# HGRN2 heads with one burst of all eight levels, and other places for splits, rests and table loads

## The reference

```python
q, fz, i, g = jnp.split(h @ w_in, [HG_FDIM, 2 * HG_FDIM, 2 * HG_FDIM + D_MODEL], axis=-1)
f = lb + (1.0 - lb) * jax.nn.sigmoid(fz)
log_f = jnp.log(jnp.maximum(f, HG_F_MIN))
k = (1.0 - lb) * jax.nn.sigmoid(-fz)
q = jax.nn.silu(q.astype(f32))
# per head, 8 heads of 128, with a state S of 128 x 128
b = jnp.cumsum(gc, axis=2)
A = jnp.einsum('bhtk,bhtsk,bhsk->bhts', qc, jnp.exp(rel), kc)     # rel = b[t] - b[s], causal
o = einsum('bhtk,bhkv->bhtv', qc * jnp.exp(b), S) + einsum('bhts,bhsv->bhtv', A, vc)
S = jnp.exp(b_last)[..., None] * S + einsum('bhsk,bhsv->bhkv', kc * jnp.exp(b_last - b), vc)
return rms_norm(o * jax.nn.sigmoid(g), g_norm) @ w_out, S
```

## Time and profile before

| | |
|---|---|
| Time, median of 3 runs (lowest, highest) | 3158.94 us (3158.48, 3159.76) |
| The profiled execution: time, span | 3158.79 us, 3157.2 us |
| Busy: PE, DVE, ACT, POOL | 97%, 61%, 37%, 4% |
| Mean granted clock of TensorE | 0.990 |

### The profile page before, as it was taken

How to read it: one execution, slowest core, us unless ns; L and a number is a source line. 1 busy time by engine, 2 the same in 40 slices (tenths; PEclk the granted TensorE clock), 3 DMA queues, 4 the chain that set the end, 5 groups by cost and what they waited for, 6 DMA issues and landing times.

```text
span 3157.2 us, 76452 instructions
## 1 busy us (share of the span) xinstructions
PE 3052.8 (97%) x31972; PEld 2858.8 (91%) x31972; DVE 1917.8 (61%) x3409; ACT 1172.0 (37%) x1971; POOL 131.4 (4%) x247
## 2 busy tenths in 40 slices
PE   8999999999999999998999998999999999999998
PEld 7998999999888999998897777999999998899998
DVE  6777654456676554555547887654555777664454
ACT  4333322223555322224536665322223333422222
POOL 0000000001332000000000000000000000000000
PEclk9999999999999999999999999999999999999999
DMA  3222222223443222222120000222222222222222
GB/s 131 102 95 70 95 87 90 84 101 99 137 129 114 88 86 94 85 97 82 61 75 12 25 26 25 87 87 93 87 95 85 89 88 99 79 84 97 80 94 74
DMA packets 104596, 269.00 MB, mean 85 GB/s; under 512 B 12802, under 2 KB 45954, under 8 KB 104146
## 3 DMA queue, kind: packets, MB, share of 16 engines
q1 hardware_dynamic: 91346, 228.54, 21.8%
q0 software_dynamic: 13056, 37.64, 3.5%
HBM read 247.61 MB, written 18.52 MB: 84 GB/s over the span
## 4 chain that ended last, share of the span: by engine, by line
PE 86%; DVE 7%; ACT 3%; DVEq 2%; issue 1%; DMA 0%; ACTq 0%; SPq 0%
PE ps L671 24%; PE ps L680 14%; PE ps L682 9%; PE ps L683 9%; PE ps L684 9%; PE ps L681 7%; PE ps L1171 3%; PE ps L1149 2%; PE ps L764 1%; PE ps L1181 1%; PE ps L997 1%; PE ps L831 1%; PE ps L1269 1%; PE ps L858 0%; PE ps L768 0%
## 5 line engine op out<-in xcount | busy, mean ns | idle before, releaser
L671 PE MATMUL ps<-arena_r 128*128 128x272 f32 x6768 | 929.8, 295 | 42.3 <-DVE arena_r L2196 19.1
L671 PEld LDWEIGHTS ps<-arena_r 128*128 128x128 f32 x6768 | 875.9, 191 | 79.5 <-issue 52.0
L1597 ACT ACTIVATE arena_r<-ring 128x1024 fp32r<-128x1024 f32 (+1 forms) x240 | 275.1, 1146 | 835.0 <-PE ps L684 820.9
L680 PE MATMUL ps<-hb_r,arena_r 128*128 128x480 f32 x1408 | 537.3, 382 | 3.4 <-DVE arena_r L2228 3.0
L682 PE MATMUL ps<-hb_r,arena_r 128*128 128x304 f32 x1408 | 427.4, 304 | 0.0
L684 PE MATMUL ps<-hb_r,arena_r 128*128 128x304 f32 x1408 | 425.9, 302 | 0.0
L683 PE MATMUL ps<-hb_r,arena_r 128*128 128x304 f32 x1408 | 425.6, 302 | 0.0
L681 PE MATMUL ps<-hb_r,arena_r 128*128 128x240 f32 x1408 | 384.0, 273 | 0.0
L2228 DVE TENSOR_TENSOR arena_r<-ring,arena_r 128x1024 fp32r<-128x1024 f32 (+1 forms) x240 | 318.4, 1327 | 49.4 <-ACT arena_r L1597 49.4
L2262 DVE TENSOR_TENSOR arena<-ps,rstd 128x544 f32<-128x544 f32 x176 | 127.5, 724 | 333.8 <-PE ps L684 333.5
L682 PEld LDWEIGHTS ps<-hb_r,arena_r 128*128 128x128 f32 x1408 | 264.6, 188 | 42.1
(11 more groups left out here) (447 smaller groups left out, 4407.6 us busy)
## 6 DMA issues: line engine op xcount, KB each, us to landing
ring<-in_w_up SPq DMA_DIRECT2D x176, 512.0 KB, 3.4
ring<-in_w_mix SPq DMA_DIRECT2D x112, 512.0 KB, 3.5
ring<-in_w_down SPq DMA_DIRECT2D x64, 704.0 KB, 4.1
arena<-in_hg_s POOLq DMA_DIRECT2D x16, 512.0 KB, 3.7
out_hg_so<-arena POOLq DMA_DIRECT2D x16, 512.0 KB, 2.9
ring<-in_w_hgout SPq DMA_DIRECT2D x16, 512.0 KB, 3.5
arena<-in_cache_k SPq DMA_DIRECT2D x128, 64.0 KB, 1.9
arena<-in_cache_v POOLq DMA_DIRECT2D x128, 64.0 KB, 2.2
```

Source lines behind the costliest of these rows:

```text
L671: mm = pe.matmul(PS[:, 2 * a + hf, 0:HALF], part[:, ws], rhs[:, o:o + HALF], start=start and n == 0, stop=stop and n == 2)
L680: pe.matmul(both(a), wide, parts[:, :, c, 0:TA], start=start, stop=False, skip_group_check=True)
L1597: act.activation(wh[n % 2][:, 0:width], ring[:, k * SLOT:k * SLOT + width], ACT.Copy)\
```

## The change

In the HGRN mixer all eight levels and the turn of the keys stand in one burst on PE, after 21 of the 32 blocks of the next head. Queries and keys are updated in place in one buffer each; before DVE overwrites a half, ACT copies it to a buffer of its level (`hg_u`), 15 copies a head. DVE's update of level n waits for ACT's copy of that half, and ACT's copy of level n+1 waits for DVE's update of level n. The values of the next head are turned at the end of a head, those of head 0 right after its projection, and the first unit of the next head waits until they are taken out (`vt_ev`). ACT also takes levels 6 and 7 out of PSUM. In the last head, eight blocks of the output projection stand before the burst.

```diff
@@ -747,6 +759,8 @@
                         if c == 0:
                             if not (head0 and k == 2):
                                 pe.wait_ge(S(L + before[k]), h + 1)
+                            if k == 0 and not head0:
+                                pe.wait_ge(S(L + "vt_ev"), h)
 
                             pe.wait_ge(S(L + "wl"), h * 4 + (KC * j + k + 1))
                         if head0 and k == 0:
...
-                    ahead(3)
-
...
+                    ahead(21)
+                    if not more:
+                        project(h, 4 * KC - 2, 4 * KC)
+                        for m, c in ((0, 0), (0, 1), (0, 2), (1, 0), (1, 1), (0, 3), (1, 2), (1, 3)):
+                            out_block(m, c)
+                    pe.wait_ge(S(L + "kept"), (h + 1) * HG_KEPT)
+                    for n in range(LEVELS):
+                        mm = level_products(n)
+                    mm.then_inc(S(L + "lvl_mm"), 1)
+                    pe.wait_ge(S(L + "lvl"), h * HG_LVL + HG_LVL - 1)
+                    for c in range(NCH):
+                        pe.transpose(PS[:, 7, c * P:(c + 1) * P], hg_ks[:, c * P:(c + 1) * P], const("ident"))
+                    pe.transpose(PS[:, 6, 3 * P:4 * P], hg_ks[:, NP_TOK:NP_TOK + P], const("ident")).then_inc(S(L + "kt_mm"), 1)
+                    ahead(2)
+                    if not more:
+                        out_block(0, 4)
+                        out_block(1, 4)
                     pe.wait_ge(S(L + "vt_ev"), h + 1)
-
-                    for j2 in range(LEVELS // 2):
-                        if j2:
-                            ahead(5)
-                        for n in (2 * j2, 2 * j2 + 1):
-                            pe.wait_ge(S(L + "lvl"), h * (LEVELS + 1) + n + 1)
...
+                    pe.wait_ge(S(L + "kt_ev"), 3 * h + 1)
+                    pe.wait_ge(S(L + "at"), 2 * h + 1)
...
+                    pe.wait_ge(S(L + "kt_ev"), 3 * h + 2)
 
...
-                    ahead(2)
+                    ahead(5)
                     if not more:
-                        out_block(0, 4)
-                        out_block(1, 4)
                         out_block(0, 5)
+                        out_block(1, 5)
                     pe.wait_ge(S(L + "s"), h + 1)
+                    pe.wait_ge(S(L + "at"), 2 * h + 2)
+                    pe.wait_ge(S(L + "kt_ev"), 3 * h + 3)
 
...
                         pe.wait_ge(S(L + "dr_v"), h + 2 + 1)
                         value_turn(h + 1, 0)
-                        ahead(4)
-                    else:
-                        ahead(6)
+                    ahead(2 if hand else 4)
                     if not more:
                         out_block(0, 6)
                         out_block(1, 6)
```

```diff
+                def first_keys(h):
+
+                    act.wait_ge(S(L + "lvl"), h * HG_LVL + 1)
+                    act.activation(hg_k0, hg_sgn, ACT.Copy, scale=scratch[:, 1:2]).then_inc(S(L + "kept"), 1)
+                    act.activation(hg_half(hg_u[1], 1, 0), hg_half(hg_sgn, 1, 0), ACT.Copy, scale=scratch[:, 1:2]).then_inc(S(L + "kept"), 1)
+
+                def kept_queries(h, n):
+                    act.wait_ge(S(L + "lvl"), h * HG_LVL + (2 if n == 1 else 2 * n - 1))
+                    act.activation(hg_half(hg_u[n], n, 1), hg_half(hg_qp, n, 1), ACT.Copy).then_inc(S(L + "kept"), 1)
+
+                def kept_keys(h, n):
+                    act.wait_ge(S(L + "lvl"), h * HG_LVL + 2 * n)
+                    act.activation(hg_half(hg_u[n], n, 0), hg_half(hg_ks, n, 0), ACT.Copy).then_inc(S(L + "kept"), 1)
...
+                    first_keys(h)
+                    if more:
                         done(base, h + 1, 0)
                         hg_split(layer, h + 1, 2)
-                        kept_halves(h, 4)
+                        kept_queries(h, 1)
+                        for n in range(2, LEVELS):
+                            kept(h, n)
                         raw(h + 1, 0, split=False)
                         done(base, h + 1, 1)
                         hg_split(layer, h + 1, 3)
-                        kept_halves(h, 6)
...
+                    else:
+                        kept_queries(h, 1)
+                        high(L, V_HG + j, o3, hh, 0)
+                        kept(h, 2)
+                        high(L, V_HG + j, o3, hh, 1)
+                        kept(h, 3)
+                        raw(h, 3)
+                        for n in range(4, LEVELS):
+                            kept(h, n)
+                            high(L, V_HG + j, o3, hh, n - 2)
+                        high(L, V_HG + j, o3, hh, KC - 2)
...
+                    act.wait_ge(S(L + "at"), 2 * h + 2)
+                    for ts in hg_blocks:
+                        cp = act.activation(hg_at[ts, :].rearrange("p (c t) -> p c t", c=NCH)[:, :, ts],
+                                            hg_atc[ts, :].rearrange("p (c t) -> p c t", c=NCH), ACT.Copy)
+                    cp.then_inc(S(L + "kt_ev"), 1)
+                    if more:
+                        raw(h + 1, 2)
...
+                    if more:
                         value_turned(h + 1, 0)
-                    elif more:
-                        raw(h + 1, 2)
+                    if not more:
+                        act.activation(c_table, scratch[:, 0:1], ACT.Sqrt)
```

The DVE function's code, with the rests and evictions between the levels:

```diff
+                def next_level(h, n, dprev, doff):
+
...
+                    dve.drain()
+                    dve.tensor_tensor(dn, dv[:, :, 0], dv[:, :, 1], ALU.mult)
+
+                    def queries():
+                        dve.wait_ge(S(L + "kept"), h * HG_KEPT + (3 if n == 1 else 2 * n))
+                        dve.tensor_tensor(hg_half(hg_qp, n, 1), hg_half(hg_qp, n, 1), dv[:, :, 0:1].to_broadcast([P, m, blk]), ALU.mult)\
+                           .then_inc(S(L + "lvl"), 1)
+
+                    def keys():
+                        if n > 1:
+                            dve.wait_ge(S(L + "kept"), h * HG_KEPT + 2 * n + 1)
+                        dve.tensor_tensor(hg_half(hg_ks, n, 0), hg_half(hg_ks, n, 0), dv[:, :, 1:2].to_broadcast([P, m, blk]), ALU.mult)\
+                           .then_inc(S(L + "lvl"), 1)
+
+                    if n < LEVELS - 1:
...
                 def mix(h, more, hand=False):
                     if more:
+                        hg_rest(layer, h + 1, 1)
                         inputs(h)
...
+                    dve.drain()
+                    decayed_queries()
+                    dprev, doff = hg_f, 0
+                    for n in range(1, LEVELS):
+                        dprev, doff = next_level(h, n, dprev, doff)
+                        if n == 1 and more:
+                            spread_values(h)
...
+                        if n == 2 and more:
+                            evict(h + 1, 0)
+                            hg_rest(layer, h + 1, 2)
+                        if not more:
+                            if n in (1, 2, 5, 6):
+                                low(L, 2 * KC * j + KC, V_HG + j, o3, hh, hl, (0, 1, None, None, 2, 3)[n - 1])
+                            if n == 3:
+                                evict(h, 3)
+                            if n == 4:
+                                hg_rest(layer, h + 1, 1)
+                    if more:
+                        evict(h + 1, 1)
+                        hg_rest(layer, h + 1, 3)
+                    else:
                         spread_values(h)
...
+                        low(L, 2 * KC * j + KC, V_HG + j, o3, hh, hl, 4)
+                    dve.wait_ge(S(L + "lvl_mm"), h + 1)
...
+                    elif not hand:
+                        hg_rest(layer, h + 1, 4)
```

```diff
-                    ahead(3, 0)
+                    ahead(2, 0)
 
                     pe.wait_ge(S("at_ev_v"), h + 1)
                     for c in range(NCH):
                         pe.transpose(PS[:, 0, c * P:(c + 1) * P], at_v[:, c * P:(c + 1) * P], ident)
                     pe.transpose(PS[:, 1, 0:P], at_v[:, NT - P:NT], ident).then_inc(S("at_vt_mm"), 1)
                     turn(1)
-                    ahead(1, 0)
...
                 act.wait_ge(S(x_sem), x0 + c + 1)
                 high("ff_", V_FFN + layer, x3, ff_hh, c)
+                if c == KC - 1:
+                    act.activation(c_table, scratch[:, 0:1], ACT.Sqrt)
 
             def after_feed_forward(layer, c):
...
+                if c == KC - 2 and (layer + 1) % 3:
+                    act.activation(c_table, scratch[:, 0:1], ACT.Sqrt)
 
             def feed_forward(layer):
                 base = UB[layer, "ff"]
...
+                    if split and not (first and k == 1):
                         done(base, h, k)
                         hg_split(layer, h, k + 2)
                     if first and k == 0:
                         root(norm_name(layer, "m"), 2)
+                        done(base, h, 1)
+                        hg_split(layer, h, 3)
                     if k == 0:
...
                         root(name_o, 2)
```

(70 more changed lines are left out.)

217 lines of the change are left out of this document (56 added, 161 removed).

## The result

The changed kernel takes 3171.53 us (median of 9 runs, 3163.82 to 3176.26), the kernel before in runs beside it 3158.48 (3154.97 to 3161.42): a ratio of 1.0042, interval 1.0033 to 1.0051, or 13 us slower. The prediction was 3148, faster. The profiled execution of the changed kernel took 3168.61 us with a span of 3167.0, 9.8 more than that of before, so most of the loss can be read in it.

A forecast was written before the change was run, and what follows sets the result against it. PE, busy 97% of the span, was taken as the bound, so only its waits and turns could be gained: 10.2 - 3.4 - 7.4 - 2.8 - 0.4 - 6.9 = -10.7, from 3158.79 to 3148.1 us; range 3133 to 3159.

The forecast's parts named there:

- The attention edits: Attention: the edits move a fraction of a microsecond each way, -0.4 us, bounds -1.5 and +1.5.
- A burst also has a start and an end of its own: HGRN heads 1 to 7: one burst saves 0.7 us of turns and up to 0.6 more; 1.2 a head taken.
- the rivals: Level chain hides, 3138 (0.18); last head cheap, 3140 (0.12); hand-over bounds heads, 3169 (0.10); RWKV gain lost, 3153.5 (0.10).
- The slower rival: HGRN heads: ACT-DVE hand-overs take 0.15 us more than counted, a head 1.5 longer, 3169 us; chance 0.10.
- the first value turn: Second HGRN head's unit 0, both layers: 2.0 us of new wait plus 1.1 for half clock, 3.1 a layer.
- the forecast's gain in the FFNs: Four FFNs: the rest goes before an eviction it need not follow, -0.7 us each, -2.8 in all.
- the period of a head: HGRN heads: near 33.85 us against 34.32, with waits near 0.4 before unit 2 and before the burst.
- the three waits: Last HGRN head: PE waits 2.3, 1.3 and 5.6 us, later 1.4; net +5.2 a layer, bounds +1 and +7.
- The output stage: HGRN output stages: shorter waits, less half clock, Sqrt's table loaded in the last head; -3.7 us a layer, -7.4.
- layer 0's start: Start of layer 0: the 1.9 us wait and the half clock behind it go, -3.4 us.
- RWKV's units 4 to 6: RWKV's start: earlier rests remove waits before units 4 and 6, and half clock; -6.9 us.
- the change in the heads: HGRN heads, per layer: -3.2 + 3.1 + 5.2 = +5.1 us, both layers +10.2.

The follow-up runs named there:

- run 1: The changed kernel with the Exp of lambda taken before the root again at the start of attention: 1.0011 against the kernel before.
- run 2: The changed kernel with the two projection blocks of attention's heads 0 to 6 back in their old places: 1.0039 against the kernel before.
- run 6: The kernel before with only the edits at stage starts and early table loads, HGRN heads and attention as before: 0.9940, 3140.58 us.
- run 5: The kernel before with only the change in HGRN's heads, including the early load of Sqrt's table in the last head: 1.0050.
- run 3: The changed kernel with one block, taken from ahead of the burst, between levels 0 to 2 and 3 to 7: 1.0061 against the kernel before.
- run 4: The kernel of run 1 with two blocks, taken from behind the burst, between levels 0 to 2 and 3 to 7: 1.0007 against the kernel before.

## Why the prediction was wrong

It had -10.7 us, and the trace has +9.8. Two steps failed, and they account for most of it.

*"The attention edits move a fraction of a microsecond each way: -0.4, bounds -1.5 and +1.5."* They cost 9.8 us (runs 1 and 2). The step names the turn of the weights as what is late next, and says nothing of ACT's order inside the loop. That order changed: entered with Sqrt's table, as it ends, the loop has its load behind the split (the kernel before, run 1); entered with that of Exp, it has the load at its top, before the split, in all seven passes.

*"A burst also has a start and an end of its own ... up to 0.6 more may go. I take 1.2 in all."* The price of a burst was taken from rows of bursts of 24 to 66 matmuls, each followed by some four microseconds of projections. Eight levels in a row stop in the middle when their code is new: 8.2 us in four bursts, and 1.55, 1.5 and 1.55 of half clock behind three of them (in layer 3 it reaches into the state's products), 12.8 in all. The cost of code that runs for the first time was put at nothing, though the waits that end with "issue" in RWKV's heads (above) stood in the trace of before. None of the rivals had it. The slower rival, a hand-over between ACT and DVE that bounds the heads, named a time near the measured one (3169), but did not come: the period is 33.91.

With -10.7, +10.2 for attention (9.8 and the 0.4 that did not come) and +12.8, and less 2.2 for the half clock that was weighed in at the first value turn and did not follow (granted 1.00 in this trace), the sum is +10.1. That this comes so near to +9.8 is partly luck. The 9.8 are a difference of medians; by the stretches of the table, attention and the FFN before it came out only 6.4 us worse than forecast (+5.3 for -1.1). The HGRN layers came out 8.6 worse (layer 0, +6.6 for -2.0) and 1.0 (layer 3 with the FFN before it, +1.7 for +0.7), and 4.6 lie elsewhere: 1.8 before RWKV's hidden layer, 1.6 in RWKV's heads, whose time varies with the clock, and 1.2 in the last stretch. There an FFN's wait of 0.7 went, yet the stretch is 0.5 longer, so the forecast's gain in the FFNs does not show.

What held: the period of a head, 33.91 for 33.87, with its two waits of 0.36 and 0.31 for 0.4 and 0.35. The first unit of the second head waits 1.89, for 2.0. The load of Sqrt's table fits into the last head: ACT still waits 1.00 for DVE behind it, before the last high part. In the last head of layer 3, which has no stall, the three waits are 2.35, 0.98 and 4.63, and a later one 1.61:

```profile
2687.62 0.99 PE L683 MATMUL ps<-arena_r 128*128 128x272 f32 x6 [2.35 <-DVE arena_r L2207]
2689.58 1.73 PE L683 MATMUL ps<-arena_r 128*128 128x272 f32 x6 [0.98 <-DVE arena_r L2207]
2695.95 3.27 PE L683 MATMUL ps<-arena_r 128*128 128x272 f32 x13 [4.63 <-DVE arena_r L2207]
```

That head lost 3.6 us by the table, and 1.5 for the two blocks that the seventh head now leaves ahead of the mark less than before: 5.1, for 5.2. (In runs 1 and 2 the same head took 2.7 and 2.5 us longer, with half clock behind that later wait.) The output stage gave 3.5 and 3.7, for 3.7; layer 0's start 3.7 (run 6), for 3.4; the stage starts together 19, for 20.5. Of RWKV's units 4 to 6 nothing waits any more, and both pairs run through (against the earlier trace rows):

```profile
1508.57 12.19 PE L683 MATMUL ps<-arena_r 128*128 128x272 f32 x96
...
1528.17 12.29 PE L683 MATMUL ps<-arena_r 128*128 128x272 f32 x96
```

So even without its two surprises the change in the heads was a loss of about 10 us, as forecast: run 1 stands 3.5 us above the kernel before although the starts give 19, and 12 of these 22.5 are the stalls and the half clock behind them.

## What to carry to other kernels

When an activation with another table is moved across the entry of a loop, look for the load in the new order of the engine: here it moved to the loop's top, and its 1.28 us became a wait of 1.46 on PE in six of the seven passes. A long run of very short matmuls can have a price where its code runs for the first time; look in the trace of before for waits that end with "issue", and weigh longer work put inside the run against what the cut costs in every other pass (here it gave back nearly all). Price edits apart where they meet: here the stage starts alone took 0.6% off, and one bundle with them lost 0.4%.

## What the runs showed of the hardware that was not expected

PE stopped 1.9 to 2.3 us in the middle of a burst of small matmuls at the code's first pass in four places (1.7 to 2.5 in runs 1, 2 and 5, which have this burst), and no later pass stopped there.

Waits of about two microseconds do not bring half clock each time. It followed three of these four stalls in the changed kernel, and two, one and one in runs 1, 2 and 5. Behind the wait of 1.89 us at the second head's first unit in layer 0 the granted clock stayed 1.00 in the changed kernel and in run 3; in runs 1, 2, 4 and 5 it was 0.56 to 0.71 over the three microseconds after the same wait.

Two blocks put into the burst cost 0.58 us a head, 0.31 at the cut and 0.27 where they were taken away; the rows of before gave 0.18 for a turn.
